# Attention outputs formed transposed, with the values as stationary operand in two 64-column halves and the reciprocal sums spread by a product

## The reference

```python
def dense_attention(q, k, v, scale):
    s = jnp.einsum('bqhd,bkhd->bhqk', q, k) * scale
    p = jax.nn.softmax(s, axis=-1)
    return jnp.einsum('bhqk,bkhd->bqhd', p, v)
# latent attention: 8 heads, q and k of 96 (64 + 32 rotary), v of 64
#   latent queries see context and latent keys (768), context queries see the context (256)
# grid (neighbourhood) attention: 8 heads of 64
#   a latent query sees an 8 x 16 window plus the context, with a position bias
m = g_mla * (o_mla @ w_o_mla) + g_fnet * (o_fnet @ w_o_fnet) + g_nat * (o_nat @ w_o_nat)
y = m @ w_out + b_out
```

## Time and profile before

| | us |
|---|---|
| median of 3 runs | 3454.34 (3452.95 to 3456.94) |
| the profiled execution | 3456.12 |
| its span on the core | 3454.3 |
| PE busy | 3011.7 (87%) |
| DVE busy | 1983.3 (57%) |
| ACT busy | 1378.9 (40%) |
| latent value products (L668) | 102.0, 832 records |

### The profile page before, as it was taken

How to read it: one execution, slowest core, us unless ns; L and a number is a source line. 1 busy time by engine, 2 the same in 40 slices (tenths; PEclk the granted TensorE clock), 3 DMA queues, 4 the chain that set the end, 5 groups by cost and what they waited for, 6 DMA issues and landing times.

```text
span 3454.3 us, 36499 instructions
## 1 busy us (share of the span) xinstructions
PE 3011.7 (87%) x13048; PEld 2127.0 (62%) x13048; DVE 1983.3 (57%) x2511; ACT 1378.9 (40%) x1614; POOL 443.5 (13%) x453
## 2 busy tenths in 40 slices
PE   4999899999988699999974499899998779999992
PEld 1545477777754577777741245478665467777771
DVE  1781466411115688888833771356111678888885
ACT  0210135411102477777730210146210257777771
POOL 1220000011115200000001420000011410000002
PEclk7999899999998699999986699999999789999996
DMA  7761000212121799999965451001333299999993
GB/s 244 238 183 34 5 1 10 72 45 72 37 106 40 246 391 393 392 392 392 392 230 183 148 178 34 5 1 33 92 103 112 76 315 391 392 392 392 391 384 110
DMA packets 379619, 660.31 MB, mean 191 GB/s; under 512 B 63002, under 2 KB 114634, under 8 KB 379122
## 3 DMA queue, kind: packets, MB, share of 16 engines
q1 hardware_dynamic: 344182, 537.05, 44.7%
q0 software_dynamic: 25824, 87.18, 7.5%
q10 hardware_dynamic: 9504, 34.61, 2.5%
HBM read 610.30 MB, written 51.31 MB: 192 GB/s over the span
## 4 chain that ended last, share of the span: by engine, by line
PE 72%; DVE 8%; issue 7%; ACT 6%; DMA 4%; POOL 1%; DVEq 0%; SPq 0%; PEldq 0%; ACTq 0%; POOLq 0%
PE slot L868 21%; PE abank L749 10%; PE abank L532 7%; PE vbank L756 6%; PE slot L799 4%; ACT round L1663 3%; PE slot L643 2%; PE vbank L668 2%; PE vbank L585 2%; PE abank L558 2%; PE vbank L570 2%; PE vbank L720 2%; DVE round L1356 2%; DVE arena L1367 1%; DMA arena<-in_w_up_e 1%
## 5 line engine op out<-in xcount | busy, mean ns | idle before, releaser
L868 PE MATMUL slot<-round,round 128*128 128x512 f32 x4608 | 1112.6, 397 | 69.4 <-DVE round L1356 65.6
L868 PEld LDWEIGHTS slot<-round,round 128*128 128x128 f32 x4608 | 859.6, 190 | 272.7 <-issue 61.2
L1348 DVE TENSOR_TENSOR round<-arena,round 128x2048 fp32r<-128x2048 f32 x384 | 873.9, 2290 | 158.6 <-ACT round L1663 157.6
L1663 ACT CAST round<-arena 128x2048 fp32r<-128x2048 f32 x384 | 734.8, 1914 | 334.6 <-PE slot L868 301.3
L749 PE MATMUL abank<-round,round 128*128 128x512 f32 (+1 forms) x1728 | 371.5, 371 | 14.7 <-DMA arena<-in_w_o_mla 14.7
L749 PEld LDWEIGHTS abank<-round,round 128*128 128x128 f32 x1728 | 292.3, 191 | 82.7 <-issue 37.6
L532 PE MATMUL abank<-arena 128*128 128x512 f32 (+1 forms) x640 | 228.5, 517 | 3.3 <-ACT arena L1479 3.3
L1614 ACT ACTIVATE arena<-abank,bT 128x512 f32<-128x512 f32 x72 | 44.4, 616 | 458.7 <-PE abank L749 458.7
L1022 DVE SCALAR_TENSOR_TENSOR arena<-arena,csT 128x512 f32<-128x512 f32 x320 | 213.3, 735 | 17.8 <-DMA y_slots<-arena 13.1
L756 PE MATMUL vbank<-arena 128*128 128x512 f32 (+1 forms) x576 | 217.9, 521 | 0.0
L1877 POOL DMA_INDIRECT arena<-h_rows,ids x64 | 79.4, 1240 | 1039.7 <-PE vbank L859 991.0
(11 more groups left out here) (236 smaller groups left out, 3377.6 us busy)
## 6 DMA issues: line engine op xcount, KB each, us to landing
arena<-in_w_gate_e SPq DMA_DIRECT2D x128, 1024.0 KB, 9.5
arena<-in_w_up_e SPq DMA_DIRECT2D x128, 1024.0 KB, 11.8
arena<-in_w_down_e SPq DMA_DIRECT2D x128, 1024.0 KB, 9.0
arena<-in_w_ada POOLq DMA_DIRECT2D x80, 512.0 KB, 4.2
y_slots<-arena ACTq DMA_DIRECT2D x66, 512.0 KB, 6.4
arena<-in_w_in SPq DMA_DIRECT2D x48, 512.0 KB, 6.0
arena<-in_w_in SPq DMA_DIRECT2D x8, 2048.0 KB, 9.9
arena<-in_w_ada SPq DMA_DIRECT2D x4, 2048.0 KB, 17.4
```

Of the source, the lines that this page charges most:

```text
L868: last = pe.matmul(out_ap, st_, w[:, k, :], start=(first and k == 0 and m == 0), stop=(final and k == 3 and m == 2))
L1348: dve.tensor_tensor(wlo[n0 % RING][:, :, :], raw[n0 % RAW][:, :, :], whi[n0 % RING][:, :, :].bitcast(F32), ALU.subtract).then_inc(lo_ready, 1)
L1663: act.copy(whi[n0 % RING][:, :, :], raw[n0 % RAW][:, :, :]).then_inc(hi_ready, 1)
```

## The change

In both attentions the values become the stationary operand (64 columns) and the transposed probabilities the moving one (128 columns), so the output comes out transposed: value dimension on the partitions, query token on the columns. Two such products are put beside each other, one into output partitions 0 to 63 and one into 64 to 127: two neighbouring query tiles of one head in the latent attention, the two heads of the pair in the grid attention. Latent `value` steps therefore come for two items at once, in every second step, and PT has four buffers instead of two.

The reciprocal of the row sum now has to vary along the columns. PE spreads it: the reciprocal of an item, repeated to 64 columns, is the stationary operand and the identity the moving one; two such products fill an abank, ACT copies it to `inv_rows` (`nat_inv_rows`), and DVE multiplies the value in the vbank with it straight into `oT_mla` (`oT_nat`), after waiting for that ACT copy. `finish_heads`, `o_mla`, `o_nat` and ACT's copies at the end go. Several buffers change their place: the oT, half of the lower part of hT, the second WO and sg.

```diff
@@ -205,12 +205,12 @@
         bin_rows, rpb_z, mod_rows = ar(110, P), ar(110.5, P), ar(111, P)
         zeros = ar(165, 512)
-        o_mla, o_nat = ar3(125, NTILES, 512), ar3(137, NTILES, 512)
         qT = [ar(0, TOK), ar(3, TOK)]
         kT = [ar(149, TOK), ar(152, TOK)]
         tb = ar(8, 512)
+        inv_rows, nat_inv_rows = [ar(10, P), ar(10, P, P)], [ar(112, P), ar(112, P, P)]
         PR = [ar(12, TOK), ar(15, TOK)]
-        PT = [ar3(18, NTILES, P), ar3(21, NTILES, P)]
+        PT = [ar3(kb, NTILES, P) for kb in (18, 21, 139, 142)]
         wuq = ar3(155, 2, HEADS * P)
...
@@ -223,7 +223,7 @@
             return w.rearrange("p (b r j) -> p r b j", r=ROWS, j=BCOL)
 
-        hT_hi, hT_los = rd3(32, KD, TOK), [rd3(125, KD // 2, TOK), rd3(155, KD // 2, TOK)]
+        hT_hi, hT_los = rd3(32, KD, TOK), [rd3(113, KD // 2, TOK), rd3(155, KD // 2, TOK)]
         hT_tmp = [rd3(149, 1, TOK), rd3(152, 1, TOK)]
...
@@ -231,10 +231,10 @@
             return hT_los[k // 4][:, k % 4, :]
 
-        oT_mla, oT_nat = ar3(113, 4, TOK), ar3(92, 4, TOK)
+        oT_mla, oT_nat = ar3(125, 4, TOK), ar3(137, 4, TOK)
         mT = ar3(68, KD, TOK)
-        WO = [ar3(104, 4, 512), ar3(137, 4, 512)]
-        sg = [ar(145, 512), ar(147, 512)]
+        WO = [ar3(104, 4, 512), ar3(92, 4, 512)]
+        sg = [ar(100, 512), ar(102, 512)]
         rows = {n: ar(92 + 4 * k, D) for k, n in enumerate(
...
@@ -369,8 +370,8 @@
                 if 1 <= i <= len(items):
                     steps.append(("turn", i - 1, *items[i - 1]))
-                if i >= 2:
-                    steps.append(("value", i - 2, *items[i - 2]))
+                if i >= 3 and i % 2:
+                    steps.append(("value", i - 3, *items[i - 3]))
                 if i % per == 1 and i // per + 1 < HEADS:
...
@@ -600,14 +602,6 @@
                     close(last, vgroups)
                 barrier("pe", pe)
-
-                def finish_heads(src, count):
-                    pe.wait_ge(vec_taken, count)
-                    for t in qt:
-                        ps = act()
-                        for k in range(4):
-                            last = pe.transpose(ps[:, k * P:(k + 1) * P], src[:, t, k * P:(k + 1) * P], ident)
-                        close(last, agroups)
 
...
@@ -660,15 +654,24 @@
                         if kind == "value":
                             _, i, h, t = step
-                            pe.wait_ge(vec_taken, turned[i][0])
-                            pe.wait_ge(act_taken, turned[i][1])
+                            pe.wait_ge(inv_ready, ib + i + 2)
+                            ps = act()
+                            for e in range(2):
+                                n = (i + e) % 4
+                                last = pe.matmul(ps[64 * e:64 * e + 64, 0:P], rinv[:, n:n + 1].to_broadcast([P, 64]),
+                                                 ident, start=True, stop=True)
+                            close(last, agroups)
+                            shares_act.append(len(agroups))
                             kt = NTILES if t >= CTX_TILES else CTX_TILES
                             ps = vec()
+                            pe.wait_ge(vec_taken, turned[i + 1][0])
+                            pe.wait_ge(act_taken, turned[i + 1][1])
                             for k in range(kt):
-                                last = pe.matmul(ps[:, 0:64], PT[i % 2][:, k, :], v[:, k, h * 64:(h + 1) * 64],
-                                                 start=(k == 0), stop=(k == kt - 1))
+                                for e in range(2):
+                                    last = pe.matmul(ps[64 * e:64 * e + 64, 0:P], v[:, k, h * 64:(h + 1) * 64],
+                                                     PT[(i + e) % 4][:, k, :], start=(k == 0), stop=(k == kt - 1))
                             close(last, vgroups)
-                    finish_heads(o_mla, len(vgroups))
+                            shares_vec.append(len(vgroups))
 
...
@@ -713,15 +716,23 @@
                             else:
                                 tiles = [t, t + 1, 0, 1] if lt >= 0 else [0, 1]
+                            pe.wait_ge(nat_inv_ready, nib + i + 1)
+                            ps = act()
+                            for e in range(2):
+                                n = 2 * (i % 4) + e
+                                last = pe.matmul(ps[64 * e:64 * e + 64, 0:P], nat_inv[:, n:n + 1].to_broadcast([P, 64]),
+                                                 ident, start=True, stop=True)
+                            close(last, agroups)
+                            nat_shares_act.append(len(agroups))
                             ps = vec()
-                            for e in range(2):
-                                h = 2 * hp + e
-                                for k, kt in enumerate(tiles):
-                                    last = pe.matmul(ps[:, 64 * e:64 * e + 64], PTn[i % 2][e][:, k, :],
-                                                     nv[:, kt, h * 64:(h + 1) * 64],
+                            for k, kt in enumerate(tiles):
+                                for e in range(2):
+                                    h = 2 * hp + e
+                                    last = pe.matmul(ps[64 * e:64 * e + 64, 0:P], nv[:, kt, h * 64:(h + 1) * 64],
+                                                     PTn[i % 2][e][:, k, :],
                                                      start=(k == 0), stop=(k == len(tiles) - 1))
                             close(last, vgroups)
-                    finish_heads(o_nat, len(vgroups))
+                            nat_shares_vec.append(len(vgroups))
 
...
@@ -1131,15 +1142,20 @@
                             _, i, h, t = step
                             ps = take()
-                            dve.tensor_copy(PT[i % 2][:, 0:2, :].rearrange("p a b -> p (a b)"), ps[:, 0:256]
+                            dve.tensor_copy(PT[i % 4][:, 0:2, :].rearrange("p a b -> p (a b)"), ps[:, 0:256]
                                             ).then_inc(vec_taken, 1)
                             dve.wait_ge(probs_ready, ib + i + 1)
-                            link(dve.reciprocal(rinv[:, i % 4:i % 4 + 1], rsum[:, i % 4:i % 4 + 1]))
+                            dve.reciprocal(rinv[:, i % 4:i % 4 + 1], rsum[:, i % 4:i % 4 + 1]).then_inc(inv_ready, 1)
                         if kind == "value":
                             _, i, h, t = step
                             ps = take()
-                            dve.tensor_scalar(o_mla[:, t, h * 64:(h + 1) * 64], ps[:, 0:64],
-                                              rinv[:, i % 4:i % 4 + 1], None, ALU.mult).then_inc(vec_taken, 1)
+                            dve.wait_ge(act_taken, shares_act[(ib + i) // 2])
+                            row = 64 * (h % 2)
+                            for e in range(2):
+                                at = slice(64 * e, 64 * e + 64)
+                                last = dve.tensor_tensor(oT_mla[row:row + 64, h // 2, (t + e) * P:(t + e + 1) * P],
+                                                         ps[at, 0:P], inv_rows[(ib + i) // 2 % 2][at, :], ALU.mult)
+                            last.then_inc(vec_taken, 1)
 
...
@@ -1173,13 +1189,17 @@
                             dve.wait_ge(nat_probs, 2 * (nib + i) + 2)
                             k = 2 * (i % 4)
-                            link(dve.reciprocal(nat_inv[:, k:k + 2], nat_sum[:, k:k + 2]))
+                            dve.reciprocal(nat_inv[:, k:k + 2], nat_sum[:, k:k + 2]).then_inc(nat_inv_ready, 1)
                         if kind == "value":
                             ps = take()
-                            for e in range(2):
-                                h, k = 2 * hp + e, 2 * (i % 4) + e
-                                last = dve.tensor_scalar(o_nat[:, t, h * 64:(h + 1) * 64], ps[:, 64 * e:64 * e + 64],
-                                                         nat_inv[:, k:k + 1], None, ALU.mult)
+                            dve.wait_ge(act_taken, nat_shares_act[nib + i])
+                            if lt == 3:
+                                places = ((0, 64, TOK - 64), (64, 64, CTX))
+                            else:
+                                places = ((0, P, t * P if lt < 0 else t * P + 64),)
+                            for at, n, to in places:
+                                last = dve.tensor_tensor(oT_nat[:, hp, to:to + n], ps[:, at:at + n],
+                                                         nat_inv_rows[i % 2][:, at:at + n], ALU.mult)
                             last.then_inc(vec_taken, 1)
...
@@ -1528,15 +1548,17 @@
                                            bias=nmx[:, k:k + 1], scale=MLA_SCALE, accum_out=rsum[:, k:k + 1]
                                            ).then_inc(probs_ready, 1)
+                        if kind == "value":
+                            p = (ib + step[1]) // 2
+                            ps = take()
```

(27 more changed lines are left out.)

## The result

The changed kernel runs in 3431.07 us (median, 3430.53 to 3431.76); the kernel before in 3453.64 us beside it. The ratio is 0.9938, with a 95% interval of 0.9927 to 0.9950. Between the medians it is 22.6 us faster; the ratio gives 21.4 us and its interval 17 to 25. The profiled execution after has a span of 3428.7 us.

The account below looks back on a forecast made before the run. TensorE was taken as the bound in all four attention stages, with a plain chain at each stage end. Savings of 7.9 + 9.1 + 2.2 + 2.9 = 22.1 us gave 3434.0 profiled, 3432 us median; forecast range 3418 to 3447.

Parts of the forecast that it names:

- Value pair: Both attentions: 24 value records for two items run side by side in 1.29 us, 2.57 us if in turn.
- The bound from the row halves (L695): Score products in two row halves: 8 records need at least 1.71 us in turn but last 1.13, so run side by side.
- A value step of 1.82 us: TensorE, six-tile pair: tiling changes 0.16 each, shares 0.21, values 1.29, in place of 2 x 1.29 us.
- Latent, layer 1: Latent stage of layer 1: seven heads save 0.65 us each, 4.5 us, and the end 4.6; 9.1 us saved.
- my chain for the end: End of layer 1's latent stage: turn, pair, turn, pair, then VectorE's product and drain; 9.55 us in place of 14.17.
- Latent, layer 0: Latent stage of layer 0: seven heads save 2.5 us and the end 5.4; 7.9 us saved.
- the three waits: Layer 0 latent head: TensorE waits 0.85, 0.45 and 0.3 us at turns, eating most of its 1.5 us saving.
- Grid loop: Grid items: VectorE's product waits for ScalarE's shares copy, delaying the next reduction; 3.94 us an item with a cast, 3.22 without.
- Ends: Grid stages, last reduction to output weights loaded: 6.75 us in place of 13.16 (layer 0), 7.25 in place of 12.17 (layer 1).
- Sum: All four stages: 7.9 + 9.1 + 2.2 + 2.9 = 22.1 us saved.
- The halves in turn: Slower rival, both attentions: column halves do not overlap, a value pair costs 1.50 us more; 3500 us, chance 0.20.
- The loop-free grid: Faster rival, grid attention: the loop is hidden, latent items go at TensorE's 3.33 us; 3411 us, chance 0.06.

Follow-up runs that it names:

- in_turn: The changed kernel with all value products of one column half issued before those of the other, in both attentions; 3464.12 us, 1.0029 of the kernel before.
- Copy_in_four: The changed kernel with ScalarE's 128-column copy of the shares cut into four of 32 columns, in both attentions; 3437.61 us.
- early_two: The changed kernel with the grid attention's shares one step early, except the first item's, and the reciprocal ahead of the split; 3418.57 us, 0.9905 of the kernel before.
- both: The changed kernel with grid shares one step earlier, reciprocal ahead of the turn copy, and the latent value pair ahead of the turn in odd steps; 3438.30 us.
- even_early: The changed kernel with early_two's grid edits and the latent value pair one step later, in even steps ahead of the turn; 3406.97 us, 0.9870 of the kernel before.

## Why the prediction was right, point by point

- **Value pair, 1.29 us: right.** Measured 1.29, and in_turn shows why. The bound from the row halves (L695) carried over to column halves. The Trainium skill's rule ("TensorE: Matmul & The Clock Gate", Part 3), that weight loads overlap a product in flight only with another row group, is not borne out here: loads of 64 columns last 0.137 us each in this trace, at 0.054 us a record, through the same 128 rows. The estimate from that page's figure for three column tiles (2.38 times, in Measured speedup) was 1.62 us a pair; the measured factor for two is 2.0, with 24 records of 0.107 us (2.57) against 1.29.
- **A value step of 1.82 us:** 1.78 as the records stand (the turn's four end at 443.84, 0.43 after 443.41, and the next score begins at 445.62). Its terms were off both ways: the change of tiling costs 0.10 to 0.12 us, not 0.16, the shares 0.27, not 0.21.
- **Latent, layer 1: forecast 9.1, measured 7.8.** Heads 15.96 against 15.85 (0.8 us over seven). The end took 10.26 us against 9.55. The step that failed is in the last rows of that stage, PE, kernel after:

```profile
2329.25 0.60 PE L651 MATMUL abank<-cst,arena 128*128 128x128 f32 x4
...
2330.43 0.44 PE L661 MATMUL abank<-cst,rinv 128*64 128x128 f32 x4 [0.58 <-DVE rinv L1148]
...
2330.70 1.48 PE L671 MATMUL vbank<-arena 128*64 128x128 f32 x24
...
2332.93 2.00 PE L698 MATMUL slot<-arena 64*128 64x256 f32 x16 [0.74 <-DVEq L340]
```

  With no further score to hide it, the last shares product waits 0.58 us for VectorE's reciprocal; my chain for the end had the turn and then the pair, without the turn copy and the reciprocal between them. Layer 0 has the same 0.58.
- **Latent, layer 0: forecast 7.9, measured 4.3,** or 6.0 with the first head alike. Heads 20.04 against 19.85; the three waits came where they were set (0.75, 0.32, 0.26 us as PE's idle time, against 0.85, 0.45 and 0.3). The end as above. The rest, 1.7 us, is the clock of the first head, which no row of before let me foresee.
- **Grid loop: right.** 3.91 us against 3.94; a head pair of layer 0 20.28 against 20.6. Ends 6.34 and 7.06 against 6.75 and 7.25. Net 3.3 and 3.0 against 2.2 and 2.9. Copy_in_four and early_two show the loop by lengthening it and by taking it away.
- **Sum: 22.1 forecast, 18.4 in the stages, 22.6 between the medians.** The mechanism was right, but the nearness of 3432 to 3431.07 is in part luck: the stages fell 3.7 us short, and the comparison of medians has some 4 us (3 by the ratio) that the traces do not place in the changed stages. The ratio's interval, 17 to 25 us, holds both. It stays open whether those 4 us are chance; the rest of the spans, which moves by 8.8 us over twelve traces, is enough to account for them.
- **Rivals.** The halves in turn would have given 3464, not 3500: the overlap at the change of halves and the waits absorb part of it. The loop-free grid gave 3419 (early_two), not 3411, with some 2 us of waits at the start of each grid stage still in it.

## What to carry to other kernels

In this kernel, products with 64 stationary columns ran side by side when their outputs lay in different column halves and neighbours alternated between them. Grouped by half, 12 or 8 records each, they lost over half of the gain; with 4 each they lost a tenth. When work leaves the bounding engine, look at what was hidden behind it: here TensorE's busy time in the four stages fell by 40.5 us and the stages by 18.4; the rest went into waits, for an exponential and for a copy at the end of another engine's queue, and two reorderings of the step list, with no work removed, gave 23.0 us more in the stages. It helped to form a result that an engine waits for late in its own step (the shares) one step earlier, and to let the bound engine ask for a copy only when it is two steps old.

## What was not expected of the hardware

- When all records of one half stand ahead of the other's, 24, 16 and 8 records take 2.22, 1.34 and 0.47 us: an overlap, by estimate from these totals, of about 3.4 records (0.37 us) at the change of halves, however many there are.
- ScalarE copies of 32 columns from PSUM follow one another at 0.06 us, against 0.28 us for one of 128 columns; cutting a copy in four costs 0.18 us.
- The same eight projections ran in 2.68 or 4.37 us, at a granted clock of 1.00 or 0.61, after the same idle time, in five and seven of twelve traces.
- The start of a grid stage with early shares ran at a granted clock of 0.50 for some microseconds in four stages (both of `both`, layer 1 of early_two, layer 0 of even_early) and at 1.00 in four others with the same code or the same waits; it cost 1.3 to 2.8 us a stage, as much as an edit was worth.
- Stretches that no kernel here changes differ by up to 8.8 us in 2990 between single traces, more than any of the four stages gained.
